# Stick-breaking attention with scanned products turned directly, steps of V, and scores in two row tiles

## The chip, the cores and the metric

One core of a Trainium2 chip runs one launch of the kernel. The metric is the device time in microseconds (us), lower is better. TensorE is called PE here, VectorE DVE, ScalarE ACT, GpSimd POOL, and SyncE SP. PSUM is the memory that PE writes to. It has eight banks of 512 float32 columns in 128 partitions.

## What is computed

One layer of a decoder for 2048 tokens of width 1024, float32: RMSNorm, a projection, two groups of attention heads, an output projection, a SwiGLU and a last RMSNorm. The change is in the second group, stick-breaking attention: 8 heads of 64, strictly causal.

```python
z = jnp.einsum('bqhd,bkhd->bhqk', qb, k) * scale
strict = key_idx[None, :] < q_idx[:, None]
log_beta = jax.nn.log_sigmoid(z)
log_1mb = jnp.where(strict, jax.nn.log_sigmoid(-z), 0.0)
later = lax.cumsum(log_1mb, axis=3, reverse=True) - log_1mb
a = jnp.where(strict, jnp.exp(log_beta + later), 0.0)
return jnp.einsum('bhqk,bkhd->bqhd', a, v)
```

With g = sigmoid(-z) and C[s] the product of g over all keys from s up to the query, the weight of key s is C[s+1] - C[s].

## The kernel before

Heads are worked in eight pairs p. Pairs 0 to 3 are the differential attention ("diff"), pairs 4 to 7 the stick-breaking one; m is 0 or 1, the head within a pair. A stick pair has 17 **pieces**. A piece is 128 queries by 1024 keys (or two query tiles that share 1024 columns), once for each m. A step e = 2i + m is one head of piece i, and the 68 pieces make 136 steps. For a step:

- `stick_scores` (L714, L716, L717) writes z into PSUM `h_z` m, in two banks of 512 columns. q and k are split in a high and a low part. k holds its high part in rows 0 to 63 and its low part in rows 64 to 127, and q holds one part in both halves of the rows, so a product over 128 rows by q high and one by q low give all four products. Where the diagonal lies in a run of columns, a 128-column product adds the mask.
- `gate` (ACT, L1096) turns z into sigmoid(-z) in place. `scan` (DVE, L1264) multiplies it up from the last key to the first, from PSUM into `h_more`. `difference` (POOL, L1364) writes C[s+1] - C[s] to `h_work`.
- `stick_turn` (L981) transposes the eight 128x128 tiles of `h_work` into `h_t`. `stick_evacuate` (ACT, L1105) copies them to `h_attn_t`. `stick_apply` (L1003) multiplies them with V into `h_o`, 64 output rows for each m.

After every fourth or fifth piece an output bank closes: `lift` (ACT), `lay` (PE, L1017), `settle` (ACT), `sum_squares` (DVE), `normalize_bank` (POOL).

Each engine runs a program of its own in a fixed order, and semaphores order them among each other. Around piece i PE does: scores of (i, m), turn of (i-2, m), half of the products with V of piece i-3, first for m = 0, then for m = 1. The scores of (i, m) wait until the scan of (i-1, m) has read `h_z` m.

In 11 of a pair's 17 pieces each bank holds one run of 512 columns. In the other six one bank holds two runs (384 and 128, or 256 and 256), as they belong to two query tiles: in three of them this is the upper bank, in three the lower. Ten of the eleven and all six hold a diagonal.

The diff part (units j) is another pipeline: PE scores, DVE `maximum` (L1178), ACT `exponential`, POOL `totals` (L1317), DVE `invert` (L1199), POOL `scale`, DVE `combine`, PE turn, ACT, PE apply. SP's queue loads the operands of pair p + 2 when pair p has been applied. `after(now)` runs side work of each engine at a given unit.

## Time and profile before

| what | value |
|---|---|
| median of 3 runs | 2861.14 us (2859.22 to 2863.82) |
| profiled execution: its own time, its span | 2860.66 us, 2858.8 us |
| PE busy | 2788.6 us, 98% of the span |
| DVE, ACT, POOL busy | 1894.1, 1471.7, 861.9 us |

The span is from the first to the last instruction of the profiled execution. Matmuls overlap in the array, so the busy time of PE includes overlap. A matmul takes weights that were loaded before it (PEld rows); the time that one costs is read from the start of one to the start of the next, not from its duration.

### The profile page before, as it was taken

What the parts mean: (1) busy time and instruction counts of PE and PEld (TensorE: products, weight loads), DVE (VectorE), ACT (ScalarE), POOL (GpSimd) and SP (SyncE); (2) the same over time, 40 slices, a digit from 0 to 9 for tenths busy, and PEclk for the clock granted to TensorE, in tenths of its full rate; (3) what the DMA queues carried; (4) which work ended last, traced back from release to release, by engine and by line L of the source; (5) the groups of instructions that cost most, each with busy time, mean ns of one, the idle gap of its engine ahead of it and who ended that gap; (6) DMA issues with size and microseconds to landing.
All of it is one profiled execution on the core that took longest, in us unless ns stands there. A gap on an engine that the chain in (4) does not pass through costs nothing.

```text
span 2858.8 us, 51825 instructions
## 1 busy us (share of the span) xinstructions
PE 2788.6 (98%) x19192; PEld 2449.8 (86%) x19192; DVE 1894.1 (66%) x2800; ACT 1471.7 (51%) x2572; POOL 861.9 (30%) x947
## 2 busy tenths in 40 slices
PE   7999999999999999999999999999999999999998
PEld 6888778878888877777899999998889998999886
DVE  6214430087777777777577877787478877878656
ACT  5112221177777666666455545554355555655444
POOL 1832222066776786776002221111100000011110
PEclk9999999999999999999999999999999999999999
DMA  5489897466554523520559999999757784899984
GB/s 195 137 191 225 211 231 170 119 156 148 113 133 107 119 60 75 119 82 16 199 164 331 323 284 289 283 285 290 197 165 235 241 252 157 256 328 300 253 230 158
DMA packets 303337, 559.42 MB, mean 196 GB/s; under 512 B 32272, under 2 KB 70160, under 8 KB 301968
## 3 DMA queue, kind: packets, MB, share of 16 engines
q1 hardware_dynamic: 262768, 463.06, 51.0%
q0 software_dynamic: 39072, 92.30, 17.4%
q8 instruction: 111, 1.82, 0.3%
q10 hardware_dynamic: 1312, 1.64, 0.2%
q14 instruction: 74, 0.61, 0.1%
HBM read 449.91 MB, written 197.13 MB: 226 GB/s over the span
## 4 chain that ended last, share of the span: by engine, by line
PE 70%; DVE 4%; DMA 2%; ACT 2%; issue 1%; POOL 1%; SPq 0%; DVEq 0%; ACTq 0%; POOLq 0%
PE f_ps L2507 26%; PE f_ps L2391 19%; PE h_z L714 5%; PE h_o L1003 5%; PE h_z L717 5%; PE h_t L981 4%; PE h_o L939 3%; PE h_t L924 2%; DVE f_wlo L1880 1%; DMA f_wraw<-sums_scratch 1%; PE h_z L716 1%; DVE h_negmax L1178 1%; PE f_ps L2431 0%; PE f_ps L2417 0%; DVE f_xsum L2093 0%
## 5 line engine op out<-in xcount | busy, mean ns | idle before, releaser
L1880 DVE TENSOR_TENSOR f_wlo<-f_wraw,f_whi 128x512 fp32r<-128x512 f32 x834 | 574.7, 690 | 234.1 <-ACT f_whi L1873 232.3
L1873 ACT ACTIVATE f_whi<-f_wraw 128x512 fp32r<-128x512 f32 x834 | 520.8, 627 | 393.8 <-PE f_ps L2507 254.3
L2507 PE MATMUL f_ps<-f_hi_s,f_whi 128*128 128x256 f32 x1408 | 391.2, 278 | 7.1 <-DVE f_up L2232 7.1
L2507 PE MATMUL f_ps<-f_lo_s,f_whi 128*128 128x256 f32 x1408 | 391.7, 278 | 0.0
L2507 PE MATMUL f_ps<-f_hi_s,f_wlo 128*128 128x256 f32 x1408 | 389.8, 277 | 0.0
L1364 POOL TENSOR_TENSOR h_work<-h_more 128x1024 f32<-128x1024 f32 (+7 forms) x192 | 264.7, 1395 | 115.6 <-DVE h_more L1264 115.6
L2507 PE MATMUL f_ps<-f_hi_a,f_whi 128*128 128x256 f32 x1056 | 292.0, 276 | 1.0 <-DVE f_second L2232 1.0
L2507 PE MATMUL f_ps<-f_hi_a,f_wlo 128*128 128x256 f32 x1056 | 291.6, 276 | 0.0
L2507 PE MATMUL f_ps<-f_lo_a,f_whi 128*128 128x256 f32 x1056 | 291.6, 276 | 0.0
L2507 PEld LDWEIGHTS f_ps<-f_hi_s,f_whi 128*128 128x128 f32 x1408 | 264.4, 188 | 8.8 <-DVE f_wlo L1880 4.4
L1264 DVE TENSOR_TENSOR_SCAN h_more<-h_z,h_zero 128x1024 f32<-128x1024 f32 (+7 forms) x128 | 231.7, 1812 | 59.4 <-ACT h_z L1096 56.9
L2507 PEld LDWEIGHTS f_ps<-f_hi_s,f_wlo 128*128 128x128 f32 x1408 | 264.8, 188 | 0.0
L2507 PEld LDWEIGHTS f_ps<-f_lo_s,f_whi 128*128 128x128 f32 x1408 | 264.4, 188 | 0.0
L1178 DVE TENSOR_REDUCE h_negmax<-h_z 128x1 f32<-128x1024 f32 (+7 forms) x192 | 169.5, 908 | 132.5 <-PE h_z L717 129.7
L2391 PE MATMUL f_ps<-f_whi,f_shi 128*128 128x512 f32 x608 | 237.3, 390 | 2.6 <-DVE f_slo L2209 2.6
L2391 PE MATMUL f_ps<-f_whi,f_slo 128*128 128x512 f32 x608 | 236.6, 389 | 0.0
L2391 PE MATMUL f_ps<-f_wlo,f_shi 128*128 128x512 f32 x608 | 236.6, 389 | 0.0
L714 PE MATMUL h_z<-h_k,h_qmain 128*128 128x512 f32 (+3 forms) x576 | 225.4, 399 | 6.9 <-ACT h_more L1050 3.9
L717 PE MATMUL h_z<-h_k,h_qmain 128*128 128x512 f32 (+3 forms) x576 | 222.0, 395 | 0.0
L1942 ACT ACTIVATE f_shi<-f_piece 128x512 fp32r<-128x512 f32 x154 | 97.4, 632 | 218.6 <-PE f_ps L2391 205.7
L1096 ACT ACTIVATE h_z<-h_z 128x1024 f32<-128x1024 f32 x136 | 137.0, 1008 | 135.1 <-PE h_z L717 135.0
L578 PE MATMUL p_ps<-p_hhi,p_whi 128*128 128x512 f32 x512 | 200.5, 392 | 1.8 <-DVE p_olo L502 1.8
(203 smaller groups left out, 6448.2 us busy)
## 6 DMA issues: line engine op xcount, KB each, us to landing
f_wraw<-in_w_stream SPq DMA_DIRECT2D x394, 256.0 KB, 4.3
f_wraw<-sums_scratch SPq DMA_DIRECT2D x352, 256.0 KB, 4.8
sums_scratch<-in_w_stream POOLq DMA_DIRECT2D x132, 256.0 KB, 5.4
act_scratch<-f_act SPq DMA_DIRECT2D x88, 256.0 KB, 4.0
combined_acts<-f_act SPq DMA_DIRECT2D x88, 256.0 KB, 5.2
f_wraw<-down_sums SPq DMA_DIRECT2D x88, 256.0 KB, 3.5
f_piece<-combined_acts SPq DMA_DIRECT2D x88, 256.0 KB, 3.1
down_sums<-in_w_stream POOLq DMA_DIRECT2D x66, 256.0 KB, 6.3
```

The lines of the kernel that those rows point to most:

```text
L578: mm = pe.matmul(bank[o % BLOCKS][:], w[s][:, c, :], h[:, c, :], start=(c == 0 and m == 0), stop=(c == KC - 1 and m == 2))
L714: pe.matmul(out, query(m, 0, seg["tile"]), keys, start=True, stop=False)
L717: mm = pe.matmul(out, query(m, 1, seg["tile"]), keys, start=False, stop=True)
L1003: mm = pe.matmul(o_bank[use % 2][own, at * P:(at + 1) * P], v_sb[s][:, seg["key_tile"] + j, own], attn_t[sticks[t["steps"][m]]["buf"]][:, ...
L1096: act.activation(z[e % 2][:], z[e % 2][:], ACT.Sigmoid, scale=-1.0).then_inc(S["gated"], 1)
L1178: done = dve.tensor_reduce(neg_max[R["set"]][:, col:col + 1], z[t["z"]][:, cols_of(seg)], AX.X, ALU.max, negate=True)
L1264: done = dve.tensor_tensor_scan(buffer[:, a:b][:, ::-1], z[m][:, cols_of(seg)][:, ::-1], zero[:].to_broadcast([P, seg["tiles"] * P]), begi ...
L1364: done = pool.tensor_tensor(work[sticks[e]["slot"]][:, cols_of(seg)], buffer[:, a + 1:b + 1], buffer[:, a:b], ALU.subtract)
L1873: act.activation(w_hi[ring][:], w_raw[ring][:], ACT.Copy).then_inc(S["hi_split"], 1)
L1880: dve.tensor_tensor(w_lo[ring][:], w_raw[ring][:], w_hi[ring][:].bitcast(F32), ALU.subtract).then_inc(S["lo_split"], 1)
L2391: mm = pe.matmul(bank[outs + t][:], a[:, tok], w[u % RING][:], start=(start and n == 0), stop=(stop and n == 2))
L2507: mm = pe.matmul(outs[i], w[ring][:, col], a[name][:, c, :], start=(c == 0 and m == 0), stop=(c == 3 and m == 2))
```

## The change

The weights are no longer formed. With V' [s] = V[s-1] - V[s] (V[-1] = 0) the sum over s of (C[s+1] - C[s]) V[s] is the sum over s of (C[s] - 1) V'[s]. So the scanned values are transposed as they are, the copy out of PSUM adds -1, POOL's `difference` is gone, and POOL makes V' once for each pair (`step_values`) from V and a copy of V that is loaded one row lower (`load_shifted`).

The gate writes to memory (`gated`), and the scan reads there. `h_z` has three slots of two banks instead of two and a separate `h_t`; scores and transposes take the slots in turn (`scores_in`, `turned_in`).

The scores of both heads of a piece are made together by products over 64 rows: head 0 in one half of the rows, head 1 in the other half (`load_crossed_keys` puts head 1's keys the other way round). Of the four partial products that of both low parts is left out, and three stay. For the third, each head changes to the other half of the rows, after a wait on the semaphore `crossed`.

PE's order around piece i is now: scores of piece i for both heads, turns of piece i-1 for both heads, `lay`, products with V of piece i-2 in one block.

```diff
+def load_crossed_keys(sp, k, qk_scratch, p, a, b, done):
+    row = rows_of(p)[1]
+    for m in range(2):
+        for part in range(2):
+            half = (part + m) % 2
+            sp.dma_start(k[half * HEAD_DIM:(half + 1) * HEAD_DIM, m, a:b].bitcast(F32),
+                         qk_scratch[part, row + m * HEAD_DIM:row + (m + 1) * HEAD_DIM, a:b]).then_inc(done, 16)
...
+def load_shifted(sp, v, v_scratch, p, done):
+    first = rows_of(p)[2]
+    rows = v_scratch[p // DIFF_PAIRS, :, first:first + COLS].rearrange("(k p) n -> p k n", p=P)
+    sp.dma_start(v[1:P], rows[0:P - 1]).then_inc(done, 16)
+    sp.dma_start(v[0:1, 1:TOK_TILES, :], rows[P - 1:P, 0:TOK_TILES - 1, :]).then_inc(done, 16)
...
+def groups_of(segs):
+    found = [[], []]
+    for bank in range(2):
+        runs = []
+        for seg in segs:
+            a, b = max(seg["at"], 4 * bank), min(seg["at"] + seg["tiles"], 4 * bank + 4)
+            if a < b:
+                first = seg["key_tile"] + a - seg["at"]
+                runs.append((seg["tile"], slice(a * P, b * P), slice(first * P, (first + b - a) * P), first + b - a == seg["tile"] + 1))
+        for n, run in enumerate(runs):
+            found[n].append((bank, run))
+    return found
...
+        scores_in, turned_in, held_by, place = {}, {}, [None, None, None], 0
+        for i in range(len(pieces) + 1):
+            for m in range(2):
+                if i < len(pieces):
+                    slot = m if i < 3 else place % 3
+                    scores_in[2 * i + m], held_by[slot] = (slot, held_by[slot]), ("gated", 2 * i + m + 1)
+                    place += 1
+            for m in range(2):
+                if i:
+                    slot = m if i < 3 else place % 3 if i < len(pieces) else 2
+                    turned_in[2 * (i - 1) + m], held_by[slot] = (slot, held_by[slot]), ("evacuated", 2 * (i - 1) + m + 1)
+                    place += 1
...
+        def stepped_at(p):
+            return diff_units + 1 + pieces_through(p - 2) + 6 if p > DIFF_PAIRS else units_through(p - 2) + 11
...
-                load_keys(sp, k_st[s], qk_scratch, p, HALF_SEQ, SEQ, late_keys[s])
-                load_keys(sp, k_st[s], qk_scratch, p, 0, HALF_SEQ, early_keys[s])
+                keys = load_keys if p < DIFF_PAIRS else load_crossed_keys
+                keys(sp, k_st[s], qk_scratch, p, HALF_SEQ, SEQ, late_keys[s])
+                keys(sp, k_st[s], qk_scratch, p, 0, HALF_SEQ, early_keys[s])
                 load_queries(sp, q_main[s], qk_scratch, p, INNER[1], LAST_TILE, INNER[1], outer[s])
                 load_queries(sp, q_main[s], qk_scratch, p, 0, INNER[0], 0, outer[s])
                 load_values(sp, v_sb[s], v_scratch, p, values[s])
+                if p >= DIFF_PAIRS:
+                    load_shifted(sp, v_step[s], v_scratch, p, values[s])
...
+                for e in t["steps"]:
+                    holder = scores_in[e][1]
+                    if holder is not None:
+                        pe.wait_ge(S[holder[0]], holder[1])
+                outs, keys, ends, rows = [ring[scores_in[e][0]] for e in t["steps"]], k_st[s], [None, None],                     (slice(0, HEAD_DIM), slice(HEAD_DIM, P))
+                def products(low, part, run):
+                    tile, cols, found, _ = run
+                    for m in range(2):
+                        own = rows[(m + low) % 2]
+                        ends[m] = pe.matmul(outs[m][:, cols], query_of(s)(m, part, tile)[own], keys[own, m, found],
+                                            start=not low and part == 0, stop=bool(low))
+                def masks(low, run):
+                    _, cols, _, diagonal = run
+                    for m in range(2 if diagonal else 0):
+                        own = rows[(m + low) % 2]
+                        pe.matmul(outs[m][:, cols.stop - P:cols.stop], ident_bf[own], strict[own], start=False, stop=False)
+                begun, (first, second) = t["crossed"], groups_of(t["segs"])
+                for _, run in first:
+                    products(0, 0, run)
+                    masks(0, run)
+                    products(0, 1, run)
+                    ends[1].then_inc(S["crossed"], 1)
+                for bank, run in first:
+                    pe.wait_ge(S["crossed"], begun + bank + 1)
+                    masks(1, run)
+                    products(1, 0, run)
+                    if second and second[0][0] == bank:
+                        ends[1].then_inc(S["crossed"], 1)
+                for _, run in second:
+                    pe.wait_ge(S["crossed"], begun + 3)
+                    products(0, 0, run)
+                    masks(0, run)
+                    products(0, 1, run)
+                    ends[1].then_inc(S["crossed"], 1)
+                    pe.wait_ge(S["crossed"], begun + 4)
+                    masks(1, run)
+                    products(1, 0, run)
+                for m in range(2):
+                    ends[m].then_inc(S["scored"], 1)
...
-                pe.wait_ge(S["multiplied"], e + 1)
-                if e:
-                    pe.wait_ge(S["evacuated"], e)
+                slot, holder = turned_in[e]
+                pe.wait_ge(S["scanned"], e + 1)
+                if holder is None:
+                    pe.wait_ge(D["evacuated"], diff_units)
                 else:
-                    pe.wait_ge(D["evacuated"], diff_units)
+                    pe.wait_ge(S[holder[0]], holder[1])
                 for j in range(CHUNK_TILES):
-                    mm = pe.transpose(t_bank[:, j * P:(j + 1) * P], work[step["slot"]][:, j * P:(j + 1) * P], ident[:])
+                    mm = pe.transpose(ring[slot][:, j * P:(j + 1) * P], work[step["slot"]][:, j * P:(j + 1) * P], ident[:])
...
-                cur, turning, applying, closing = piece_at(i), piece_at(i - 2), piece_at(i - 3), closing_at(i - 4)
-                if cur is None and turning is None:
-                    pe.wait_ge(S["scanned"], len(sticks))
-                    ahead()
+                cur, turning, applying, closing = piece_at(i), piece_at(i - 1), piece_at(i - 2), closing_at(i - 3)
+                if cur is not None:
+                    stick_scores(cur)
                 for m in range(2):
-                    if cur is not None:
-                        stick_scores(cur, m)
                     if turning is not None:
                         stick_turn(sticks[turning["steps"][m]])
-                    if applying is not None:
-                        stick_apply(applying, m)
-                    if m == 0 and closing is not None:
-                        lay(closing)
+                    if turning is pieces[-1] and m == 0:
+                        pe.wait_ge(S["evacuated"], len(sticks) - 2)
+                        ahead()
+                if closing is not None:
+                    lay(closing)
+                if applying is not None:
+                    stick_apply(applying)
...
-                act.activation(z[e % 2][:], z[e % 2][:], ACT.Sigmoid, scale=-1.0).then_inc(S["gated"], 1)
+                if e >= 2:
+                    act.wait_ge(S["scanned"], e - 1)
+                act.activation(gated[e % 2][:], ring[scores_in[e][0]][:], ACT.Sigmoid, scale=-1.0).then_inc(S["gated"], 1)
...
-                act.activation(attn_t[step["buf"]][:], t_bank[:], ACT.Copy).then_inc(S["evacuated"], 1)
+                act.activation(attn_t[step["buf"]][:], ring[turned_in[e][0]][:], ACT.Identity, bias=minus_one[:]).then_inc(S["evacuated"], 1)
...
-                m = e % 2
+                m, held = e % 2, work[sticks[e]["slot"]]
                 dve.wait_ge(S["gated"], e + 1)
-                if e >= 2:
-                    dve.wait_ge(S["multiplied"], e - 1)
+                if e >= 4:
+                    dve.wait_ge(S["transposed"], e - 3)
                 for seg in t["segs"]:
-                    buffer, a, b = shadow(seg, m)
                     begin = 1.0
                     if not seg["opens"]:
-                        begin = buffer[:, b:b + 1]
+                        begin = work[sticks[e - 2]["slot"]][:, 0:1]
                         dve.wait_ge(S["scanned"], e - 1)
-                    done = dve.tensor_tensor_scan(buffer[:, a:b][:, ::-1], z[m][:, cols_of(seg)][:, ::-1],
+                    done = dve.tensor_tensor_scan(held[:, cols_of(seg)][:, ::-1], gated[m][:, cols_of(seg)][:, ::-1],
                                                   zero[:].to_broadcast([P, seg["tiles"] * P]), begin, ALU.mult, ALU.add)
...
-            def difference(e, t):
-                if e >= 4:
-                    pool.wait_ge(S["transposed"], e - 3)
-                elif e == 0:
-                    pool.wait_ge(D["combined"], diff_units)
-                pool.wait_ge(S["scanned"], e + 1)
-                for seg in t["segs"]:
-                    buffer, a, b = shadow(seg, e % 2)
-                    done = pool.tensor_tensor(work[sticks[e]["slot"]][:, cols_of(seg)], buffer[:, a + 1:b + 1], buffer[:, a:b], ALU.subtract)
-                done.then_inc(S["multiplied"], 1)
+            def step_values(p):
+                s = p % 2
+                pool.wait_ge(values[s], 16 * DIFF_PAIRS // 2 + 48 * (p // 2 - DIFF_PAIRS // 2 + 1))
+                chain(pool.memset(v_step[s][0:1, 0, :], 0.0))
+                pool.tensor_tensor(v_step[s][:], v_step[s][:], v_sb[s][:], ALU.subtract).then_inc(S["stepped"], 1)
...
+                for p in range(DIFF_PAIRS, PAIRS_OF_MAPS):
+                    if stepped_at(p) == now:
+                        step_values(p)
```

PE's program, one half of a piece with its diagonal in a 128-column run, before (`h_t` is the transposes' PSUM, `h_o` the output bank):

```order
L714 MATMUL h_z<-h_k,h_qmain 128x512 [waits h_s_scanned]
L717 MATMUL h_z<-h_k,h_qmain 128x512
L714 MATMUL h_z<-h_k,h_qmain 128x384
L717 MATMUL h_z<-h_k,h_qmain 128x384
L714 MATMUL h_z<-h_k,h_qmain 128x128
L716 MATMUL h_z<-strict,ident_bf 128x128
L717 MATMUL h_z<-h_k,h_qmain 128x128
L981 MATMUL h_t<-ident_sb,h_work 128x128 [waits h_s_evacuated,h_s_multiplied]
L981 MATMUL h_t<-ident_sb,h_work 128x128 x7
L1003 MATMUL h_o<-h_attn_t,h_v 64x128 [waits h_o_copied,h_s_evacuated,h_values1]
L1003 MATMUL h_o<-h_attn_t,h_v 64x128 x7
```

In the changed kernel a whole piece of this kind stands like this; the rows end ahead of its last mask and product:

```order
L1033 MATMUL h_z<-h_k_49,h_qmain_52 128x512 [waits h_s_evacuated,h_s_gated]
L1033 MATMUL h_z<-h_k_49,h_qmain_52 128x512 x3
L1033 MATMUL h_z<-h_k_49,h_qmain_52 128x384 x4
L1033 MATMUL h_z<-h_k_49,h_qmain_52 128x512 [waits h_s_crossed]
L1033 MATMUL h_z<-h_k_49,h_qmain_52 128x512
L1033 MATMUL h_z<-h_k_49,h_qmain_52 128x384 [waits h_s_crossed]
L1033 MATMUL h_z<-h_k_49,h_qmain_52 128x384
L1033 MATMUL h_z<-h_k_49,h_qmain_52 128x128 [waits h_s_crossed]
L1033 MATMUL h_z<-h_k_49,h_qmain_52 128x128
L1040 MATMUL h_z<-strict,ident_bf 128x128 x2
L1033 MATMUL h_z<-h_k_49,h_qmain_52 128x128 x2
L1040 MATMUL h_z<-strict,ident_bf 128x128 [waits h_s_crossed]
```

Seven products and masks for each head have become 22 of half the rows for both heads, with four waits on `crossed` among them, of which the last two stand directly behind the product that they wait for. Behind the scores PE's rows are now these (turn, turn, apply):

```order
L1075 MATMUL h_z<-ident_sb,h_work 128x128 [waits h_s_evacuated,h_s_scanned]
L1075 MATMUL h_z<-ident_sb,h_work 128x128 x7
L1075 MATMUL h_z<-ident_sb,h_work 128x128 [waits h_s_gated,h_s_scanned]
L1075 MATMUL h_z<-ident_sb,h_work 128x128 x7
L1094 MATMUL h_o<-h_attn_t,h_vstep 64x128 [waits h_s_evacuated]
L1094 MATMUL h_o<-h_attn_t,h_vstep 64x128 x15
```

The second turn waits for `gated`, which before stood on no row of PE; each head's turn had its own apply behind it.

POOL's program in the last diff pair (p = 3), before:

```order
L1332 TENSOR_SCALAR h_more<-h_more,h_factor,h_neglam 128x1024
L1332 TENSOR_SCALAR h_more<-h_more,h_factor,h_neglam 128x512
L1332 TENSOR_SCALAR h_more<-h_more,h_inverse,h_neglam 128x512
L1311 TENSOR_TENSOR h_shift<-h_negall,h_negmax 128x4
L1317 TENSOR_TENSOR h_total<-h_sum,h_weight 128x4
L1318 TENSOR_TENSOR h_both<-h_total 128x2
L1324 TENSOR_TENSOR h_factor<-h_weight,h_inverse 128x4
```

and in the changed kernel:

```order
L1413 TENSOR_SCALAR h_more<-h_more,h_factor,h_neglam 128x1024
L1413 TENSOR_SCALAR h_more<-h_more,h_factor,h_neglam 128x512
L1413 TENSOR_SCALAR h_more<-h_more,h_inverse,h_neglam 128x512
L1392 TENSOR_TENSOR h_shift<-h_negall,h_negmax 128x4
L1442 MEMSET h_vstep 1x128
L1443 TENSOR_TENSOR h_vstep<-h_vstep,h_v_50 128x2048
L1398 TENSOR_TENSOR h_total<-h_sum,h_weight 128x4
L1399 TENSOR_TENSOR h_both<-h_total 128x2
L1405 TENSOR_TENSOR h_factor<-h_weight,h_inverse 128x4
```

Between the shift and the totals of one round now stand the clearing and the subtraction that make V' for pair 4.

## Rows read from the trace of the kernel before

**Rows 1.** The page: busy us (share of the span) and instructions of each engine.
```profile
PE 2788.6 (98%) x19192; PEld 2449.8 (86%) x19192; DVE 1894.1 (66%) x2800; ACT 1471.7 (51%) x2572; POOL 861.9 (30%) x947
```

**Rows 2.** Windows: stretch, its us, busy us (instructions) by engine, PE clock, DMA.
```profile
1100.00:1200.00 100.00, 100.00 (x941) 79.42 (x940) 74.13 (x47) 67.11 (x79) 70.24 (x57) 1.00 0.37 85
1200.00:1300.00 100.00, 100.00 (x949) 79.88 (x945) 75.32 (x48) 66.24 (x75) 72.61 (x59) 1.00 0.21 70
```

**Rows 3.** Timeline, half a piece without mask: start, us, engine, line, operation.
```profile
1136.89 0.50 PE L714 MATMUL h_z<-h_k,h_qlast 128*128 128x512 f32 x1
...
1137.23 0.40 PE L717 MATMUL h_z<-h_k,h_qlast 128*128 128x512 f32 x1
...
1137.69 0.39 PE L717 MATMUL h_z<-h_k,h_qlast 128*128 128x512 f32 x1
...
1137.92 1.04 PE L981 MATMUL h_t<-ident_sb,h_work 128*128 128x128 f32 x8
1138.12 1.01 ACT L1096 ACTIVATE h_z<-h_z 128x1024 f32<-128x1024 f32 x1 [1.07 <-PE h_z L717]
...
1138.89 0.85 PEld L1003 LDWEIGHTS h_o<-h_attn_t,h_v 128*64 128x64 f32 x16 [0.17 <-issue]
1138.89 1.09 PE L1003 MATMUL h_o<-h_attn_t,h_v 128*64 128x128 f32 x16
...
1139.17 2.35 DVE L1264 TENSOR_TENSOR_SCAN h_more<-h_z,h_more,h_zero 128x1024 f32<-128x1024 f32 x1 [0.73 <-ACT h_z L1096]
...
1139.91 0.50 PE L714 MATMUL h_z<-h_k,h_qlast 128*128 128x512 f32 x1
```

**Rows 4.** Timeline: short runs and their weight loads, the next two half pieces.
```profile
1120.63 0.19 PEld L714 LDWEIGHTS h_z<-h_k,h_qmain 128*128 128x128 f32 x1 [0.17 <-issue]
...
1120.74 0.19 PEld L717 LDWEIGHTS h_z<-h_k,h_qmain 128*128 128x128 f32 x1
...
1120.85 0.19 PEld L714 LDWEIGHTS h_z<-h_k,h_qmain 128*128 128x128 f32 x1
...
1123.89 0.50 PE L714 MATMUL h_z<-h_k,h_qmain 128*128 128x512 f32 x1
...
1127.05 0.50 PE L714 MATMUL h_z<-h_k,h_qmain 128*128 128x512 f32 x1
```

**Rows 5.** Timeline: from the last stick scores to the output projection.
```profile
1346.65 1.03 PE L981 MATMUL h_t<-ident_sb,h_work 128*128 128x128 f32 x8
...
1353.89 1.02 ACT L1105 ACTIVATE h_attn_t<-h_t 128x1024 f32<-128x1024 f32 x1 [0.21 <-PE h_t L981]
...
1355.06 1.06 PE L981 MATMUL h_t<-ident_sb,h_work 128*128 128x128 f32 x8 [0.18 <-ACT h_attn_t L1105]
...
1361.25 1.97 PE L1003 MATMUL h_o<-h_attn_t,h_v 128*64 128x128 f32 x32
...
1363.15 1.53 PE L2417 MATMUL f_ps<-ident_sb,f_natural 128*128 128x128 f32 x12
...
1364.87 0.49 PE L2391 MATMUL f_ps<-f_whi,f_thi 128*128 128x512 f32 x1
```

**Rows 6.** Timeline of POOL, then of DVE, in the last diff pair.
```profile
882.14 0.64 POOL L1311 TENSOR_TENSOR h_shift<-h_negall,h_negmax 128x4 f32<-128x4 f32 x1 [1.61 <-DVE h_negall L1185]
884.45 0.20 POOL L1317 TENSOR_TENSOR h_total<-h_sum,h_weight 128x4 f32<-128x4 f32 x1 [1.67 <-ACT h_weight L1074]
...
885.02 0.18 DVE L1199 RECIPROCAL h_inverse<-h_both 128x4 f32<-128x4 f32 x1 [0.39 <-POOL h_both L1318]
```

**Rows 7.** The load of V for pair 4, and a window behind its issue.
```profile
L700 SPq DMA_DIRECT2D h_v<-v_scratch x1: 597/597/597, 866.8 to 866.8; - x1
...
DMA to landing us min/median/max: 17.6/17.6/17.6
...
885.00:890.00 5.00, 5.00 (x39) 4.38 (x38) 3.98 (x5) 3.98 (x10) 3.95 (x4) 1.00 0.96 211
```

**Rows 8.** Groups by shape: POOL's `difference` at its largest size.
```profile
L1364 POOL TENSOR_TENSOR h_work<-h_more 128x1024 f32<-128x1024 f32 x80 | 151.2, 1893 | 74.4 <-DVE h_more L1264 74.4
```

114 lines of the change are left out of this document (47 added, 67 removed).

## The prediction

> **What bounds the kernel now.** I read the page first: PE is busy for 98% of the span [rows 1], so what PE does, or waits for, is the time. The windows say the same of the stretch that the change touches: from 1100 to 1300 us, in the middle of the stick phase, PE is busy without a gap and DVE for three quarters [rows 2]. POOL's `difference` is large there, but nobody on PE's path waits for it, so taking it away gives nothing by itself. The timeline then shows what PE's time consists of. In a half piece without a mask [rows 3] the first product begins at 1136.89, the second 0.34 later, the next two each 0.23 after that (1137.23 to 1137.69), the transposes at 1137.92, the sixteen products with V at 1138.89 and the next scores at 1139.91: 0.34 + 3 x 0.23 = 1.03 for scores, 0.97 to turn, 1.02 to apply, 3.02 in all. So a product of 512 columns costs 0.23, and the first one 0.11 more, which I call a switch. With a mask a half piece takes 3.16, one with a short run 3.26 [rows 4]; the mask is worth 0.13. In the same rows the weight loads of short runs start 0.11 apart: a run of 128 columns costs its load. PE is full, but a product's price is the larger of its columns and its load.
>
> **The change part by part.**
>
> *Scores, eleven full pieces of each pair.* Before, a piece makes 8 products of 512 columns, now 12 of half the rows. Nothing in the trace has two row tiles side by side, so a pair of them (one for each head) costs between 0.23, if they run together, and 0.46, if they don't. Two loads at 0.11 fill 0.22, so they fit under 0.23. I take 0.23, because the two use different rows and different PSUM. That is six pairs, 1.38. Add one switch 0.11 and two pairs of masks at 0.13 each, 0.26. The wait on `crossed` behind the second bank has one pair under it (0.23, from 0.11 on), while a product's duration is 0.39 and a handoff between engines 0.04 to 0.15 (below): 0.43 to 0.54 against 0.33, so it costs 0.1 to 0.2, say 0.15. Scores are 1.90 against 2 x (3.16 - 1.99) = 2.34 before.
>
> *Scores, six pieces with a short run.* Here each pair on a short run costs two loads, 0.22, whatever its columns. Three pairs of 512 are 0.69, six short pairs 1.32, masks 0.26, a switch 0.11. Where the short second run is in the upper bank, two waits on `crossed` come directly behind the product that they wait for, in the lower bank one. Such a wait empties the array: at least the 0.17 by which a product's duration exceeds its slot (0.40 - 0.23), at most that, the 0.15 of a handoff and a load of 0.11 twice, some 0.5. I take 0.35, as the handoff will count but not all loads. Upper: 2.38 + 0.10 + 0.70 = 3.18. Lower: 2.38 + 0.15 + 0.35 = 2.88. Before they took 6.32 to 6.52 for the whole piece, mean 6.42.
>
> *Turns.* The transposes and copies are as many as before, but the second turn gets the PSUM slot that head 0's scores have just been written to, so it waits for that gate. Nothing covers this but the first turn. From the start of head 0's last product: 0.39 until it has ended, 0.04 until the gate starts (1138.08 to 1138.12), 1.01 of gate [rows 3], 0.15 until PE starts (1354.91 to 1355.06 at the end of the phase [rows 5]), in sum 1.59. The first turn is through after 0.34 + 0.97 = 1.31, so PE idles 0.28. From the end of the scores to the end of the second turn it is 1.59 + 0.97 - 0.34 = 2.22 against 1.94.
>
> *Products with V.* 32 in one block take 1.90 (1361.25 to 1363.15 [rows 5]), against 2 x 1.02.
>
> *The sum of a piece.* Full with mask: 1.90 + 2.22 + 1.90 = 6.02 against 6.32, without mask 5.76 against 6.04, so -0.3 for each of eleven. Upper short run: 3.18 + 4.12 = 7.30 against 6.42, +0.88 for each of three. Lower: 7.00, +0.58 for each of three. For a pair -3.3 + 2.64 + 1.74 = +1.1, and **+4** for the four pairs.
>
> *What hides DVE and ACT.* Two scans at 2.35 are 4.7 [rows 3] beneath 5.76, so DVE is no bound; reading from memory where it read PSUM could even cost 20% (5.6). ACT's four passes of 1.02 are 4.1. The copy that adds -1 is the same pass. If PE fell to 4.7 per piece, DVE would be next.
>
> *V' for pair 4.* This stands on POOL in the diff phase, where it is not idle work. POOL has its shift done at 882.8 and begins the next totals at 884.45, and DVE's reciprocal waits for them 0.39 [rows 6]; DVE's maxima of the next round, and by them the exponentials and PE's scores, are queued behind it. In the changed program POOL must first have V and the shifted V. V is issued at 866.8 and lands 17.6 later, at 884.4; the shifted copy is 1.05 MB more at the 211 GB/s of that window [rows 7], 5.0 us, so 889.4. The subtraction of 2048 columns costs twice the 1.89 of 1024 [rows 8], 3.8. The totals then start at 893.2, 8.7 late, of which DVE has 0.4 to spare: **+8.4**. From below, if both land together, 3.3. From above, if the shifted V lands last (the window from 885 to 890 is still full, and 5 us come on top, 895), 14. For pairs 5 to 7 POOL waits likewise, but there only the normalizing of a bank stands behind it, which has some four pieces of time. The smaller, doubled key loads keep their bytes.
>
> *The end of the phase.* From the last scores' end, where the transposes start at 1346.65, to the first product of the output projection at 1364.87 it is 18.2 [rows 5]. With one piece less in flight what remains is: two turns 2.2, apply 1.9, a turn 1.0, the 16 transposes of the projection's input 1.9, a turn 1.0, two applies 3.8, 12 transposes 1.5, `lay` 0.5, in sum 13.8. **-4** (none to -6). The start of the phase is filled by the same units; I take nothing there.
>
> Together +4.3 + 8.4 - 4.4 = +8.3. The profiled execution took 2860.66, 0.5 below the median of the runs; I set 2869 for the median.
>
> **The rivals.** *Row tiles are cheaper than their bounds (faster).* If the loads of the two tiles overlap, a short pair costs 0.11 to 0.17, mean 0.14: 6 x 0.08 x 24 pieces = -12. If a wait on `crossed` costs only the 0.17, 36 of them give -6, and if the one in full pieces costs nothing, 68 x 0.15 = -10. All of it gives 2841, half of it 2855; I call this case 2850. It decides from about -14 on. Against it speaks that the sixteen loads of 64 columns in the column tiles of apply take 0.85 [rows 3], 0.05 each, one behind the other; for it, that those two use the same rows. The Trainium skill (TensorEngine Tiling (Array Packing), Key Properties) says that different tiles can execute loads and products in parallel. By that rule the short pairs alone would bring the sum to 2857; the apply rows disagree with it or are too short to show it. The same section says that a change of tiling mode drains the array, and the 0.11 of the first product [rows 3] agrees in kind.
>
> *Row tiles run one after the other (much slower).* A pair of 512 then costs 0.46. A pair of heads has 66 + 18 of them, +19.3, and the runs of 384 add 1.4: +83 for the phase, 2952. No row excludes it, since the column tiles' 0.06 per product fit both ways.
>
> *POOL's wait is not felt (no change).* If loads land earlier and DVE and PE have more slack than the row shows, only 0 to 3 of the 8.4 remain: 2861 to 2864.
>
> **How the numbers follow.** Forecast (2867 to 2890) 0.40, cheap tiles 0.32, serial tiles 0.10, hidden POOL wait 0.18. A measurement tells some 0.2% from no change, 5.7 us. Faster is the second case, 0.32. Same is the last one and the lower edge of the first, 0.20. Slower is the rest of the first and the third, 0.48. The range goes from the second case's all-in end, 2842, to the forecast with its upper costs (waits at 0.5: +5, POOL +6, switch and masks of row tiles dearer: +17), 2898. What it leaves out is the serial case and a little at both ends, 0.15 to 0.2. The forecast's own range is 2860 to 2885.
>
> **What the profile after would show.** Product pairs on L1033 start every 0.23 (0.46 would prove the serial case), short ones every 0.22. PE is idle some 0.3 before every second turn, released by the gate, and ACT's gate begins right behind the scores. Some 36 gaps of 0.2 to 0.5 stand before L1033 or L1040, released by PE itself. POOL's subtraction in pair 3 ends near 893, with a hole on DVE and PE of about 8 us there. The stick phase from the first gate to the last is some 4 us longer than before, and POOL is almost empty in it. I would be wrong if pairs cost clearly more or less than 0.23, if the second turn doesn't wait, or if the diff phase ends when it did.

## The result, and the profile after

The changed kernel takes 2973.52 us (median of 4 runs, 2970.29 to 2974.02) against 2862.48 (4 runs, 2859.22 to 2871.84): 1.038 times the time, interval 1.0354 to 1.0406. The profiled execution took 2973.34, with a span of 2971.5. Two anchors in the traces divide the 112.7 us between the spans. The first masked product of the stick phase (`strict`) starts at 912.50 before and at 973.21 after; the first product of the output projection starts at 1364.87 and at 1476.80. So the part ahead of the stick phase is 61 us longer, the stick phase 51 us (503.6 against 452.4), and the rest is equal within 1 us.

The page, first line of its busy times (share of the span, instructions):

```profile
PE 2779.8 (94%) x19640; PEld 2436.7 (82%) x19640; DVE 1896.9 (64%) x2797; ACT 1477.4 (50%) x2572; POOL 649.0 (22%) x763
```

PE is as busy as before within 9 us [rows 1], so what is new is idle time of PE. The windows (stretch, its us, busy us of each engine, PE clock, share of the DMA engines, GB/s) show the largest piece:

```profile
890.00:900.00 10.00, 0.53 (x5) 0.29 (x3) 0.00 (x0) 0.00 (x0) 0.00 (x0) 0.74 0.07 19
900.00:910.00 10.00, 0.00 (x0) 0.00 (x0) 0.00 (x0) 0.00 (x0) 0.00 (x0) 0.50 0.07 19
...
930.00:940.00 10.00, 0.00 (x0) 0.00 (x0) 0.00 (x0) 0.00 (x0) 1.53 (x2) 0.50 0.52 115
940.00:950.00 10.00, 3.43 (x14) 3.02 (x15) 4.84 (x7) 3.81 (x9) 7.45 (x7) 0.50 0.38 84
```

For some 40 us nothing runs but a transfer at 19 GB/s, with a DMA share of 0.07: one sixteenth is 0.0625, so one of the 16 engines is moving and fifteen are not. Before, the window behind the issue of V moved 211 [rows 7]. The timeline of the same place, first SP's queue, then POOL, then PE (start, us, engine, line, operation; the bracket is the idle time ahead and its releaser):

```profile
870.44 8.76 SPq L712 DMA_DIRECT2D h_vstep<-v_scratch  x1
879.25 54.35 SPq L713 DMA_DIRECT2D h_vstep<-v_scratch  x1
933.64 2.58 SPq L683 DMA_DIRECT2D h_qmain<-qk_scratch  x4
...
883.65 0.65 POOL L1392 TENSOR_TENSOR h_shift<-h_negall,h_negmax 128x4 f32<-128x4 f32 x1 [1.60 <-DVE h_negall L1274]
938.39 0.19 POOL L1442 MEMSET h_vstep<- 1x128 f32 x1 [54.09 <-DMA h_vstep<-v_scratch]
938.66 4.49 POOL L1443 TENSOR_TENSOR h_vstep<-h_vstep,h_v 128x2048 f32<-128x2048 f32 x1
943.11 0.20 POOL L1398 TENSOR_TENSOR h_total<-h_sum,h_weight 128x4 f32<-128x4 f32 x1
...
946.57 0.58 PE L733 MATMUL h_z<-h_k,h_qmain 128*128 128x256 f32 x1 [56.04 <-ACT h_more L1140]
```

L712 is the transfer of the shifted V over 127 partitions, L713 the small one over a single partition behind it. The second issue is held for 54.35 us. POOL, at L1442, waits in order for both; the totals of the last diff pair (L1398) stand behind it and start at 943.11 where they started at 884.45 [rows 6]. They release DVE's reciprocal, which releases the maxima, these the exponentials, and these at last PE's scores: PE is idle for 56.04 us. Four us into this idle time PE's granted clock falls from 2.4 to 1.2 GHz (0.50 in the windows), and it is back 6 us behind its end. The whole diff phase is 62 us longer than before.

The waits view from 920 to 1450 (who waits for whom: us in total, times, longest):

```profile
POOL h_vstep L1442 <- DMA h_vstep<-v_scratch: 137.5, 2, 83.4
...
POOL h_more L1442 <- DMA h_more<-v_scratch: 130.8, 2, 76.1
...
DVE h_ssumsq L1360 <- POOL h_out L1457: 55.5, 3, 37.0
PE h_z L1075 <- DVE h_work L1352: 49.2, 5, 33.1
...
PE h_z L1075 <- ACT h_more L1188: 13.6, 61, 1.2
```

The same happens to pairs 5, 6 and 7: POOL waits 76.1, 83.4 and 54.7 us for the shifted V. There it carries the normalizing of closed banks. The timeline before pair 6, on POOL, DVE and PE, shows who needed that:

```profile
1222.74 0.20 POOL L1442 MEMSET h_vstep<- 1x128 f32 x1 [83.37 <-DMA h_vstep<-v_scratch]
...
1230.88 0.69 DVE L1360 TENSOR_REDUCE h_ssumsq<-h_squares 128x8 f32<-128x512 f32 x1 [36.99 <-POOL h_out L1457]
1231.48 4.46 DVE L1352 TENSOR_TENSOR_SCAN h_work<-h_more,h_zero 128x1024 f32<-128x1024 f32 x2
...
1233.82 1.97 PE L1075 MATMUL h_z<-ident_sb,h_work 128*128 128x128 f32 x8 [33.09 <-DVE h_work L1352]
```

DVE's sum of squares of the next bank (L1360) must wait until the bank before is normalized, and the scans are queued behind it in order: PE stands still for 33.09 us. The periods from one piece's apply to the next are 6.0 to 6.8 us elsewhere; at these three places they are 21.1, 41.6 and 9.3 + 7.9, together 54 us too much.

Between these stalls the steady state can be read. A full piece with mask, then one with a short run in the upper bank, on PE:

```profile
1141.56 0.96 PE L1033 MATMUL h_z<-h_k,h_qmain 64*128 64x512 f32 x6
1142.37 0.23 PE L1040 MATMUL h_z<-strict,ident_bf 64*128 64x128 bf16 x2
...
1143.41 1.09 PE L1075 MATMUL h_z<-ident_sb,h_work 128*128 128x128 f32 x8
1144.69 1.06 PE L1075 MATMUL h_z<-ident_sb,h_work 128*128 128x128 f32 x8 [0.18 <-ACT h_more L1188]
1145.68 1.97 PE L1094 MATMUL h_o<-h_attn_t,h_more 128*64 128x128 f32 x32
1147.58 1.86 PE L1033 MATMUL h_z<-h_k,h_qmain 64*128 64x512 f32 x14
...
1149.80 0.23 PE L1040 MATMUL h_z<-strict,ident_bf 64*128 64x128 bf16 x2
...
1150.19 1.09 PE L1075 MATMUL h_z<-ident_sb,h_work 128*128 128x128 f32 x8
```

It answers to [rows 3, 4]. Scores 1.85, from their end to the end of the second turn 2.27, apply 1.90: 6.02. The short piece has 2.61 of scores. A whole pair, from the transposes of a closing to those of the same closing in the next pair, takes 107.4 us where no stall is in it; before it took 109.2.

### The profile page after: what moved, and what is told of

Read it like the earlier page. It is cut to its first block, busy times and chain, and to the rows that moved or that the text cites. A ratio compares the mean times of both kernels' runs of the same rounds, so it can differ in the third digit from the quotient of the medians.

```text
span 2971.5 us, 52610 instructions
## 1 busy us (share of the span) xinstructions
PE 2779.8 (94%) x19640; PEld 2436.7 (82%) x19640; DVE 1896.9 (64%) x2797; ACT 1477.4 (50%) x2572; POOL 649.0 (22%) x763
## 4 chain that ended last, share of the span: by engine, by line
PE 61%; another core or an unknown queue 7%; DVE 4%; ACT 3%; POOL 2%; issue 2%; DMA 1%; DVEq 0%; SPq 0%; ACTq 0%; POOLq 0%
PE f_ps L2585 26%; PE f_ps L2469 18%; PE h_o L990 3%; PE h_o L1094 3%; PE h_z L1033 3%; PE h_z L736 2%; PE h_z L733 2%; PE h_z L1075 2%; PE h_z L975 2%; ACT h_more L1188 1%; DVE h_work L1352 1%; DVE f_wlo L1958 1%; DMA f_wraw<-in_w_stream 1%; DVE h_negmax L1267 1%
## 5 line engine op out<-in xcount | busy, mean ns | idle before, releaser
L1352 DVE TENSOR_TENSOR_SCAN h_work<-h_more,h_zero 128x1024 f32<-128x1024 f32 (+7 forms) x128 | 233.0, 1844 | 46.4 <-ACT h_more L1188 46.4
L1188 ACT ACTIVATE h_more<-h_z 128x1024 f32<-128x1024 f32 x136 | 132.3, 1022 | 181.0 <-PE h_z L1033 124.1
L1075 PE MATMUL h_z<-ident_sb,h_work 128*128 128x128 f32 x1088 | 151.4, 284 | 64.6 <-DVE h_work L1352 49.2
L2585 PEld LDWEIGHTS f_ps<-f_hi_a,f_whi 128*128 128x128 f32 x1056 | 198.3, 188 | 3.3 <-DVE f_wlo L1958 1.1
L578 PE MATMUL p_ps<-p_hlo,p_whi 128*128 128x512 f32 x512 | 199.3, 389 | 0.0
```

Of the source, the lines that this page charges most:

```text
L578: mm = pe.matmul(bank[o % BLOCKS][:], w[s][:, c, :], h[:, c, :], start=(c == 0 and m == 0), stop=(c == KC - 1 and m == 2))
L1075: mm = pe.transpose(ring[slot][:, j * P:(j + 1) * P], work[step["slot"]][:, j * P:(j + 1) * P], ident[:])
L1188: act.activation(gated[e % 2][:], ring[scores_in[e][0]][:], ACT.Sigmoid, scale=-1.0).then_inc(S["gated"], 1)
L1352: done = dve.tensor_tensor_scan(held[:, cols_of(seg)][:, ::-1], gated[m][:, cols_of(seg)][:, ::-1], zero[:].to_broadcast([P, seg["tiles"] ...
L2585: mm = pe.matmul(outs[i], w[ring][:, col], a[name][:, c, :], start=(c == 0 and m == 0), stop=(c == 3 and m == 2))
```

## The experiments

Times of single executions of one kernel differ by more than 20 us: the ten of e4_shift_128_later go from 2860.39, with a mean granted clock of 0.996, to 2883.71 with 0.990. Where PE runs at a lower clock differs between the traces, also where the programs are still alike: from 560 to 600 us the mean granted clock is 1.00 before and in e5, 0.91 in the changed kernel and in e4, and 0.87 in e1. So below each median stands with its ratio to before, measured at the same time, and edits in the stick phase are compared by the trace as well: by the time of a pair (as above, 17 pieces without a stall), and by the whole stick phase between the two anchors.

| kernel | median us (runs) | ratio to before, 95% | stick phase | a pair |
|---|---|---|---|---|
| before | 2862.48 (4) | 1 | 452.4 | 109.2 |
| after | 2973.52 (4) | 1.038 (1.0354 to 1.0406) | 503.6 | 107.4 |
| e1_shift_by_128 | 2876.24 (6) | 1.0044 (1.0017 to 1.0071) | 456.6 | 107.4 |
| e2_shift_112_15 | 2877.06 (1) | | 457.6 | |
| e3_127_from_0 | 2979.80 (1) | | | |
| e4_shift_128_later | 2869.71 (10) | 1.0031 (1.0014 to 1.0049) | 461.9 | 107.4 |
| e5_full_rows | 2854.08 (10) | 0.9973 (0.995 to 0.9995) | 442.8 | 103.5 |
| e6_apply_between | 2855.88 (10) | 0.9991 (0.9972 to 1.0009) | 442.6 | 103.6 |
| e8_step_late | 2925.76 (1) | | 455.1 | |
| e9_high_first | 2853.75 (10) | 0.9963 (0.9948 to 0.9979) | 452.7 | 104.5 |
| e7_in_parts | 2837.93 (5) | 0.9916 (0.9887 to 0.9944) | 432.2 | 103.5 |
| e10_slot_sooner | 2853.89 (10) | 0.9973 (0.9959 to 0.9988) | 443.8 | |
| e11_row_tiles_mended | 2833.21 (6) | 0.9903 (0.9879 to 0.9927) | 423.7 | 100.7 |
| e12_full_rows_mended | 2837.36 (6) | 0.9907 (0.9892 to 0.9923) | 433.9 | 102.7 |

**Why is the transfer slow?** My theory was the number of partitions; the rivals were the small transfer, the source's offset by a row, and the start at partition 1. e1_shift_by_128 takes tiles 1 to 15 over all 128 partitions:

```
-    sp.dma_start(v[1:P], rows[0:P - 1])
-    sp.dma_start(v[0:1, 1:TOK_TILES, :], rows[P - 1:P, 0:TOK_TILES - 1, :])
+    low = v_scratch[p // DIFF_PAIRS, P - 1:SEQ - 1, first:first + COLS].rearrange("(k p) n -> p k n", p=P)
+    sp.dma_start(v[:, 1:TOK_TILES, :], low)
+    sp.dma_start(v[1:P, 0:1, :], rows[0:P - 1, 0:1, :])
```

> The changed kernel, with only the shifted load of V in another cut: tiles 1 to 15 as one transfer over all 128 partitions, tile 0 as one over 127 partitions (65 KB). Theory A, from the trace after: the transfer over 127 partitions (1.04 MB) runs on one of the 16 DMA engines, because 127 rows aren't shared out; it moves 19 GB/s at a DMA share of 0.07, which is 1/16, and takes some 60 us. Then here the large one runs at over 200 GB/s (5 us), the small one takes 3 to 4 us, POOL's wait for pair 4 shrinks from 54 to some 8 us, those for pairs 5 to 7 reach PE no longer, and the total falls by 95 to 110 us to 2862 to 2876. Rival B: the transfer into one partition (7.5 KB) is what is slow, SP is held 54 us at it; then this falls as well, so the next run must tell. Rival C: reading V a second time, at an address one row off, is slow in itself; then this stays near 2973.

e2_shift_112_15 leaves the small transfer alone and splits the large one into 112 and 15 partitions:

```
-    sp.dma_start(v[1:P], rows[0:P - 1])
+    sp.dma_start(v[1:P - 15], rows[0:P - 16])
+    sp.dma_start(v[P - 15:P], rows[P - 16:P - 1])
```

> The changed kernel, the transfer over partitions 1 to 127 cut in two: 112 partitions (7 x 16) and 15; the one into partition 0 stays as it is. Theory A: 112 partitions are shared by all engines (0.9 MB, 5 us), 15 are not (0.12 MB on one engine, 6 us), the total falls to 2865 to 2885. Rival B (the transfer into one partition is slow): it stays near 2973. Rival C (source one row off): near 2973. A rival D, that starting at partition 1 is slow: near 2973.

e3_127_from_0 keeps 127 partitions, but from partition 0 on and from an unshifted source:

```
-    sp.dma_start(v[1:P], rows[0:P - 1])
-    sp.dma_start(v[0:1, 1:TOK_TILES, :], rows[P - 1:P, 0:TOK_TILES - 1, :])
+    sp.dma_start(v[0:P - 1], rows[0:P - 1])
+    sp.dma_start(v[P - 1:P], rows[P - 1:P])
```

> The changed kernel with the shift left out of the copy of V: 127 partitions from partition 0 on, then partition 127 by itself, so V' is zero and the stick heads are wrong; all else is as before. Theory A (127 is not shared out): the large transfer again takes 50 to 60 us and the total stays at 2965 to 2980. Rival D (a start at partition 1 is slow) or C (an address one row off): the total falls to 2862 to 2885.

The first two are rid of the slow transfer (2876.24, a fall of 97 us that ends just at the upper edge of what I expected, and 2877.06), the third, which leaves out the shift, is not (2979.80). A window of e3, columns as above:

```profile
900.00:910.00 10.00, 0.00 (x0) 0.00 (x0) 0.00 (x0) 0.00 (x0) 0.00 (x0) 0.50 0.07 19
```

Still 19 GB/s. Neither the start, nor the source, nor the small transfer counts, only the 127. Both 128 and 112 + 15 partitions are fast: from 880 to 890 us, with V and the shifted V on their way, e2 moves 187 and 223 GB/s in its two windows of 5 us and e1 262 and 302. The Trainium skill states it (DMA: Bandwidth & Descriptors, section on why a DMA increments its semaphore by 16): the number of engines is the largest one up to 16 that divides the outermost sizes, and it names 127 partitions as a case of one engine. All three runs and the share of 0.07 agree. By the same rule 15 partitions are shared out too, over 15 engines, and not held on one, as I had expected for e2; no run here tells the two apart. I had not weighed the rule in the prediction.

In e1 POOL still waits, as the timeline at pair 4 shows:

```profile
887.77 0.65 POOL L1393 TENSOR_TENSOR h_shift<-h_negall,h_negmax 128x4 f32<-128x4 f32 x1 [1.59 <-DVE h_negall L1275]
895.92 0.20 POOL L1443 MEMSET h_vstep<- 1x128 f32 x1 [7.50 <-DMA h_vstep<-v_scratch]
896.20 4.50 POOL L1444 TENSOR_TENSOR h_vstep<-h_vstep,h_v 128x2048 f32<-128x2048 f32 x1
900.65 0.20 POOL L1399 TENSOR_TENSOR h_total<-h_sum,h_weight 128x4 f32<-128x4 f32 x1
```

The shift is done at 888.4, V' at 900.65, the totals follow. That is the case for which the prediction had its 8.4.

**Where should V' of pair 4 stand?** e4_shift_128_later is e1 with this subtraction moved behind the diff phase's last unit:

```
-            return ... if p > DIFF_PAIRS else units_through(p - 2) + 11
+            return ... if p > DIFF_PAIRS else diff_units
```

> The first of these runs, and V' for pair 4 is made on POOL in unit 68 (the end of the differential part) in place of unit 62. By my prediction the wait and the subtraction in unit 62 cost 8.4 us there, so this run is 6 to 10 us faster than the first one and ends at 2854 to 2866. Rival: with the load repaired the subtraction's place does not matter, POOL's lateness is taken up by slack, and the two agree within 3 us.

The median falls by 6.5, but it ends at 2869.71, above the 2854 to 2866 that I expected, and the intervals of the two ratios overlap, so the times alone don't decide between the theory and its rival. The traces do so for the diff phase: from its first masked product (`causal`) to the anchor it has 349.7 us against 360.3 in e1, PE's wait of 9.4 us is gone, and the longest that is left is 2.2. But the stick phase of e4 is 5.3 longer than that of e1: the subtraction now meets the first scan, which takes 5.70 us where it has 2.29 in e1 (more at e7). So part of the cost has moved there. The 349.7 are still 9.5 more than before (340.2). This isn't V' but the clock of this execution: from 560 to 850 us PE is at half clock for 20.4 us, which costs it half of them, against 3.4 before, and e5, with the same program in this phase but for the form of the key loads, has 341.1.

**Does the slow transfer hurt by itself for pairs 5 to 7, or only by POOL's order?** e8_step_late is the changed kernel with its slow transfer, where POOL is sent to the subtraction eight pieces later:

```
-            return diff_units + 1 + pieces_through(p - 2) + 6 if p > DIFF_PAIRS else ...
+            return diff_units + 1 + pieces_through(p - 2) + 14 if p > DIFF_PAIRS else ...
```

> The changed kernel as it was, with the slow transfer over 127 partitions left in, and one change: for pairs 5 to 7 GpSimd is sent to the subtraction at the 14th piece of the pair ahead instead of the 6th. Theory A, the transfer is harmful there only because GpSimd waits for it 76 and 83 us in order, with the normalizing of closed banks queued behind, which then holds VectorE's scans: the stalls of TensorE ahead of pairs 5, 6 and 7 (about 15, 35 and 4 us) all but go, the 56 us of pair 4 stay, and the time is 2915 to 2932. Theory B, the loss comes from the transfer itself (it fills one DMA queue, and loads behind it come late): the time stays within 10 us of 2973.

2925.76 in its one execution: theory A. The waits of PE for the diff exponentials (pair 4, as before) and for the scans:

```profile
PE h_z L733 <- ACT h_more L1140: 57.5, 1, 57.5
...
PE h_z L1075 <- DVE h_work L1352: 3.9, 4, 1.2
```

The 49.2 us that PE waited for scans are 3.9, the stick phase is 455.1, 48.5 shorter. The transfer takes as long as it did; nobody is queued behind it.

**What do the row tiles bring?** e5_full_rows is e4 with the old scores (all else of the change stays):

```
-                keys = load_keys if p < DIFF_PAIRS else load_crossed_keys
+                keys = load_keys
...
-                (products(), masks() and the waits on S["crossed"])
+                for m in range(2):
+                    score_matmuls(pe, ring[scores_in[t["steps"][m]][0]], query_of(s), k_st[s], m, t["segs"],
+                                  (ident_bf, strict)).then_inc(S["scored"], 1)
```

> The kernel of e4 (shifted copy over 128 partitions, V' of pair 4 later) with the scores of the stick-breaking pairs done as before the change: four products of 128 rows for each head and bank instead of six of 64 rows in two row tiles, keys loaded uncrossed, no waits on the crossing. Everything else of the change stays. Read from periods between the first apply products of neighbouring pieces: e4 has 6.02 us for a full piece, 6.67 for one with a short run in the upper bank, 6.45 to 6.47 with one in the lower bank, and 107.2 for a whole pair. Theory A, row tiles are where the steady gain comes from and the rest of the rebuilding gives nothing in steady state: full piece 6.22 (before 6.31, and the scores of two halves were 2.06 there against 1.86 now), lower short run 6.2 to 6.3, a pair 109 +-0.4, and the time 5 to 10 us above e4. Theory B, row tiles are eaten up by the waits at the crossings and the gain comes from blocks of 16 transposes and 32 applies: full piece 6.02 or less, short runs about 6.1, a pair under 107, the time below e4.

Theory A falls: the ratio drops by 0.6%, with intervals that do not overlap, and a pair from 107.4 to 103.5. The numbers are those of theory B. A full piece with mask on PE:

```profile
1167.65 0.50 PE L734 MATMUL h_z<-h_k,h_qmain 128*128 128x512 f32 x1
...
1169.55 0.48 PE L737 MATMUL h_z<-h_k,h_qmain 128*128 128x512 f32 x1
1169.86 1.91 PE L1040 MATMUL h_z<-ident_sb,h_work 128*128 128x128 f32 x16
1171.70 1.97 PE L1059 MATMUL h_o<-h_attn_t,h_vstep 128*64 128x128 f32 x32
1173.60 0.50 PE L734 MATMUL h_z<-h_k,h_qmain 128*128 128x512 f32 x1
```

Scores are 2.21, 0.36 more than with row tiles. But the turn is one row of 16 without a wait, 1.84, where it was 2.27: now head 0's scores are ready 1.1 us before head 1's, so its gate runs beneath head 1's products. With row tiles both heads are ready only at the end, and the second turn waits. The full piece is 5.95 against 6.02, and pieces with a short run are 5.97 to 6.18 against 6.44 to 6.78: six such pieces, times half a microsecond, are most of the 3.9 of a pair. So the waits at the crossings, to which theory B gave the whole loss, explain the short pieces (e9 tests it), and the wait for the gate explains the full ones (e6 tests it). In the changed kernel the row tiles lose, and the rest of the rebuilding (blocks of transposes and applies, one less piece in flight) gives 109.2 - 103.5 = 5.7 us a pair; no run divides it among these.

**The two kinds of waits of the row tiles.** e6_apply_between is e4 with apply between the two turns:

```
                 for m in range(2):
                     if turning is not None:
                         stick_turn(sticks[turning["steps"][m]])
...
-                if closing is not None:
-                    lay(closing)
-                if applying is not None:
-                    stick_apply(applying)
+                    if m == 0 and closing is not None:
+                        lay(closing)
+                    if m == 0 and applying is not None:
+                        stick_apply(applying)
```

> The kernel of e4 with one change in the order on the TensorE queue: transposes of head 0, then the apply of the piece before (and the closing transposes), then transposes of head 1. In e4 the transposes of head 1 wait 0.17 to 0.18 us of idle time for the gate in 60-odd pieces. Theory A, that wait is only a matter of order: with 1.9 us of apply ahead of the second transposes it goes, a full piece takes 5.8 instead of 6.02, and the kernel is 10 to 15 us faster than e4. Theory B, it only moves, since the scores of the next piece need the buffer that the second transposes free late and the ScalarE queue is in its old order: full piece 6.0 or more, time within 3 us of e4 or above.

Theory A: the ratio falls by 0.4% to 0.9991, some 11 us. The turn of head 1 has no bracket any more:

```profile
1170.26 1.97 PE L1095 MATMUL h_o<-h_attn_t,h_vstep 128*64 128x128 f32 x32
1172.16 1.09 PE L1076 MATMUL h_z<-ident_sb,h_work 128*128 128x128 f32 x8
1173.18 0.97 PE L1034 MATMUL h_z<-h_k,h_qmain 64*128 64x512 f32 x6
```

The second turn starts 1.90 behind the products with V, with no wait between. A full piece takes 5.80, a pair 103.6 instead of 107.4.

e9_high_first is e4 with the high products of all runs first, then the low ones:

```
                 for n, (bank, run) in enumerate(runs):
                     products(0, 0, run, banks.index(bank) == n)
                     masks(0, run)
                     products(0, 1, run)
                     ends[1].then_inc(S["crossed"], 1)
                 for n, (bank, run) in enumerate(runs):
                     pe.wait_ge(S["crossed"], begun + len(banks) - banks[::-1].index(bank))
                     masks(1, run)
                     products(1, 0, run, bank not in banks[n + 1:])
```

> The kernel of e4 with another order of the score products where a bank holds two runs: the high products of all runs first, then the low ones (the start flag is then set at the first run of a bank alone), so that two of the four waits on the crossing go. It touches 6 of 17 pieces of a pair; full pieces keep their order. Theory A, the excess of pieces with a short run over full ones (0.65 us in the upper bank, 0.43 in the lower, of which closing banks are no part) is mostly those two waits of 0.27 to 0.31: it falls by 0.4 to 0.6, a pair by 2.5 to 3.5 us, the kernel by 8 to 14 us against e4. Theory B, the excess is the narrow products themselves, which cost 0.2 for 128 columns about as for 512: it falls by less than 0.15 and the time stays within 3 us of e4.

Theory A again. From the start of a short piece's scores to its turn:

```profile
1174.96 1.08 PE L1034 MATMUL h_z<-h_k,h_qmain 64*128 64x512 f32 x10
...
1176.91 1.09 PE L1067 MATMUL h_z<-ident_sb,h_work 128*128 128x128 f32 x8
```

That is 1.95 for a piece with two runs of 256 columns in the upper bank, where the same piece has 2.51 in e4. Its period falls from 6.67 to 6.12, only 0.10 above a full one, so each of the two waits was worth 0.28. And the masks being as many as in a full piece, three pairs of 512 columns (0.69) and 0.10 pay for six pairs of 256: 0.13 for such a pair, below the 0.22 of two loads [rows 4]. The loads of the two row tiles overlap. The Trainium skill says so (TensorEngine Tiling (Array Packing), Key Properties), and with the waits out of the way the trace agrees. The medians fall by 16 us, more than the 11.6 that four pairs of 2.9 give and than the 8 to 14 that I expected; no run tells where the rest comes from.

**Why do pieces last 2 to 4 us longer while POOL subtracts?** In e5 three pieces take 7.20, 8.82 and 8.78 us, where their like in other pairs have 5.95, 6.39 and 6.40, so 6.1 us in all (the 6.7 in the expectation below compares two of them with pieces of another kind). POOL and DVE at the first of them:

```profile
975.43 0.19 POOL L1407 MEMSET h_more<- 1x128 f32 x1 [33.37 <-DMA h_more<-v_scratch]
975.71 4.71 POOL L1408 TENSOR_TENSOR h_more<-h_more,h_v 128x2048 f32<-128x2048 f32 x1
...
977.96 3.54 DVE L1317 TENSOR_TENSOR_SCAN h_work<-h_more,h_work,h_zero 128x512 f32<-128x512 f32 x1 [1.92 <-ACT h_more L1153]
...
982.54 1.25 DVE L1317 TENSOR_TENSOR_SCAN h_work<-h_more,h_work,h_zero 128x512 f32<-128x512 f32 x1
```

The scan of 512 columns, 1.25 us at 982.54, takes 3.54 and ends about when the subtraction does. Before, `difference` ran beside the scans, and of the 72 scans of 1024 columns with that form none took more than 2.29; but that scan read PSUM. e7_in_parts is e5 with the subtraction in eight parts:

```
-                pool.tensor_tensor(v_step[s][:], v_step[s][:], v_sb[s][:], ALU.subtract).then_inc(S["stepped"], 1)
+                for part in range(8):
+                    own = slice(2 * part, 2 * part + 2)
+                    done = pool.tensor_tensor(v_step[s][:, own, :], v_step[s][:, own, :], v_sb[s][:, own, :], ALU.subtract)
+                done.then_inc(S["stepped"], 1)
```

> The kernel of e5 with GpSimd's subtraction of a pair (128x2048) cut into eight of 128x256. In the profile of e5 the scans of VectorE that run while GpSimd subtracts take 4.3 to 4.4 us longer than their like (in e4: 5.80 for 128x640 against 1.46, 8.81 for two of 128x1024 against 4.47), and the pieces there last 7.20, 8.82 and 8.78 us where the others of their kind have 5.96, 5.97 and 6.17: 6.7 us in all. Theory A, one instruction with two inputs from memory on VectorE and one on GpSimd exclude each other for as long as an instruction lasts: in parts a scan waits for at most one part, about 0.6 us, the three long pieces shrink to within 0.7 of their like, and the time falls by 4 to 7 us. Theory B, both only share a rate, or the eight parts each take a turn with the scan held: the long pieces stay within 1 us of what they were. On before the scan had one input from memory and one from PSUM, so neither is seen there.

```profile
973.78 9.73 POOL L1410 TENSOR_TENSOR h_more<-h_more,h_v 128x256 f32<-128x256 f32 x8
...
976.38 1.78 DVE L1317 TENSOR_TENSOR_SCAN h_work<-h_more,h_work,h_zero 128x512 f32<-128x512 f32 x1 [1.91 <-ACT h_more L1153]
978.09 1.69 DVE L1317 TENSOR_TENSOR_SCAN h_work<-h_more,h_zero 128x512 f32<-128x512 f32 x1
```

Now each scan of 512 columns takes 1.7 to 1.8, half a microsecond for one part, and the eight parts take 9.73 where one instruction took 4.71: they take turns. The three long pieces are 6.05, 6.39 and 6.40, and the head of the phase, where the subtraction for pair 4 met the first scans (8.74 us for two), is 4.7 shorter. The stick phase falls by 10.6 us, more than I expected, since I had not counted the head. The ratio falls by 0.6%, some 16 us, of which the trace shows these 10.6. The Trainium skill has the rule (SBUF — State Buffer, section on the two separate sides): VectorE with two operands from SBUF and GpSimd hold one pair of ports in turn, each for a whole instruction. The traces agree in both directions: POOL's multiplications of 256 columns (`h_out` by `h_srstd`) all take 0.61 us before; in e4 their mean is 1.83 and the longest takes 2.59. This is what "scan from memory" cost, and the prediction had looked for it in the scan's own duration, where it isn't (2.29 us for 1024 columns where POOL is quiet, as before).

**The head of the phase.** e10_slot_sooner is e5 with the ring's third buffer used from piece 2 on:

```
-                    slot = m if i < 3 else place % 3
+                    slot = m if i < 2 else place % 3
```

> The kernel of e5 with the third PSUM buffer given to the transposes one piece sooner at the head of the stick-breaking phase (the turns of piece 1 go to it instead of waiting for the gates of piece 2). In e5 TensorE waits 4.70, 0.25, 0.15 and 2.27 us in the first four pieces, and then runs at half clock for some us. Theory A, the ring of only two buffers in these pieces makes the head long: the 2.27 goes and the head is 2 to 4 us shorter, the time as much. Theory B, the 2.27 is the wait of ScalarE's evacuation for the last apply of the difference attention (5.18 us there), which this does not touch, and the 4.70 is the scan of piece 0: within 1.5 us of e5 in the head.

In the head theory A holds in part: the wait of 2.27 is not gone but 1.4, and the second period 9.41 instead of 11.97, so from the anchor to the second apply 31.8 us instead of 35.0. The long wait at its start (4.70) does not change. ScalarE in e5 shows what it is:

```profile
917.83 1.02 ACT L1153 ACTIVATE h_more<-h_z 128x1024 f32<-128x1024 f32 x1 [4.08 <-DVE h_work L1317]
```

The gate of piece 1 waits 4.08 us for the scan of piece 0, whose buffer it needs. In the median nothing is seen (2853.89 against 2854.08), where 2 to 4 us less were expected: its profile has 4.1 us more in the pieces with a subtraction, so the times cannot tell 2 or 3 us here.

**All of it together.** e11_row_tiles_mended has the edits of e4, e6, e7, e9 and e10; e12_full_rows_mended has them with the old scores (so without e9).

> All of the change kept, row tiles too, with the mended edits together: shifted copy over 128 partitions, V' of pair 4 later, high products first, apply between the two transposes, the subtraction in eight parts, the third buffer a piece sooner. From the traces: e6 has 103.6 us for a pair and e9 took 0.55 us off each of six pieces of it, so 100.3 to 100.8 for a pair against 109.1 before and 105.9 for e5 with 128-row scores. Theory A, the savings add, since each goes at a wait of its own on TensorE: 2825 to 2842. Theory B, with these waits gone VectorE's scans (some 75 to 78 us busy of 100) or ScalarE's order set the pace: a pair of 102.5 or more and 2843 to 2856.

> The kernel of e11 with the scores as before the change (four products of 128 rows for each head and bank, no row tiles, no waits on the crossing), all else alike: what the row tiles are worth once the waits around them are gone. In e7, with 128-row scores and transposes of both heads in a row, a full piece takes 5.95 us and a pair 103.5; e11 has 5.80 and 100.7. Theory A, in the order with apply between the transposes 128-row scores change nothing, since there was no gate wait left to cover: a pair 103.2 to 103.7, and 6 to 12 us above e11, so the row tiles are worth 0.15 us for a full piece. Theory B, the gain of e11 over e7 is the order alone: a pair 101 or less, and the time within 3 us of e11.

e11 has theory A: 2833.21, 0.9903 of before. A piece whose closing follows:

```profile
1134.73 0.96 PE L1034 MATMUL h_z<-h_k,h_qmain 64*128 64x512 f32 x6
...
1136.57 1.09 PE L1067 MATMUL h_z<-ident_sb,h_work 128*128 128x128 f32 x8
...
1138.03 1.97 PE L1086 MATMUL h_o<-h_attn_t,h_vstep 128*64 128x128 f32 x32
1139.93 1.09 PE L1067 MATMUL h_z<-ident_sb,h_work 128*128 128x128 f32 x8
```

A full piece takes 5.80 and a pair 100.7: 107.4 - 3.8 (e6) - 2.9 (e9) = 100.7, so the savings add. In e12 a pair takes 102.7, between my two theories: the order gives 0.8 to the old scores too, and the row tiles are worth 2.0 us a pair, 8 for the four. The stick phases of the traces differ by 10.2 (433.9 and 423.7), the rest lying in the head and where scans meet subtractions. The medians differ by 4 and the intervals of the ratios overlap, so the whole times alone don't show it.

## Why the prediction was wrong, step by step

**The step that failed** is in "V' for pair 4": "the shifted copy is 1.05 MB more at the 211 GB/s of that window [rows 7], 5.0 us, so 889.4". I took the rate of a window full of other transfers for a transfer of another shape. It measured 54 to 59 us at 19 GB/s, and the wait on PE 56.0 in place of 8.4. From the same number follows the second half of the error: "for pairs 5 to 7 POOL waits likewise, but there only the normalizing of a bank stands behind it, which has some four pieces of time". With a fast transfer it held: in e1 POOL still waits there, up to 36 us, and PE stands for scans 5.5 us in all. With 83 us of wait it did not, and behind the normalizing stood DVE's next sum and behind that the scans: 54 us. That 56 and 54 make 110 of the 111 us between the medians is partly luck, as 8.4 of the 56 were forecast and the other terms below nearly cancel. What the transfer cost is read from e1, which differs from the changed kernel in it alone: 97 us. e1 has 2876.24, within 8 us of the forecast and within its range.

**V' for pair 4, with a transfer that all engines share**, was priced about right: PE waits 9.4 us in e1, against 8.4. Its subtraction takes 4.50 where I had 3.8.

**Scores in full pieces:** 1.85 against my 1.90. A pair of row tiles runs together, at 0.23; the serial case fell. **The turn:** 2.27 against 2.22, with the wait for the gate as told, a bracket of 0.18 beside later starts. **Apply:** 1.90 as told. The whole piece was 6.02, as computed; without mask 5.86 against 5.76.

**Short runs** were mis-sized: 2.50 to 2.61 of scores in the upper bank and 2.28 to 2.44 in the lower, against 3.18 and 2.88. A short pair of 256 columns costs 0.13 (e9), not 0.22; a wait on `crossed` 0.28, not 0.35. So the steady state was 1.8 us a pair faster, -7.3 for four in place of +4. This was the first rival's mechanism: some 11 of the 28 us that it had listed.

**The end of the phase:** from the last scores to the projection 15.1 us (1461.74 to 1476.80) against 18.2; I had 13.8. -3.1 in place of -4.4.

**The start of the phase**, where I took nothing, was mis-sized as well: the apply of the second piece starts 33.0 us behind the anchor in e1, 27.2 before. e1's stick phase is 4.2 longer than before; with -7.3 for the steady part, -3.1 for the end and +6.5 for the three collisions of subtraction and scan, some +8 are left for it. In the trace of e1 PE waits 6.0 us there against 2.3 before, and it is granted half clock for 10.3 us against 3.4, of which half is lost: 3.7 and 3.4 us, together 7 of the 8. The collisions themselves stand in no term.

So that e1 comes near the sum is luck: its steady state is 11 us better than told, and a head and collisions of 15 us were not told at all.

**What the profile after would show:** right for the 0.23 of pairs, PE's bracket ahead of each second turn and POOL nearly empty; wrong for the end of the subtraction (943, not 893), for the hole (56, not 8) and for the stick phase (51 us longer, not 4). The gaps at the crossings stand before weight loads of PEld, not before products: from 920 to 1450 us there are 60, 16 us in all, the longest 0.5.

## What to carry to other kernels

Read the shape of a new transfer before its bytes: a load over 127 partitions ran at 19 GB/s with the share of one engine in 16, and the same bytes over 128, or over 112 and 15, did not. Ask of every wait that is moved to an idle engine what stands behind it in order, and for how long it can stand: for pairs 5 to 7 the same slow transfers cost 49 us or nothing, by the place of one wait. And where a step makes two results ready at once instead of one after the other, count who worked on the first beneath the second: the row tiles saved 0.36 us of products and lost 0.43 in the turn behind them, until the order was turned.

## What the runs showed of the hardware

- A transfer over 127 partitions ran at 19 GB/s with a DMA share of 0.07, from partition 0 as well as from partition 1 (after, e3), and over 128 or 112 + 15 partitions at the rate of the rest, 187 to 302 GB/s in the windows from 880 to 890 (e1, e2).
- A scan with its inputs in memory and a POOL operation with two inputs in memory exclude each other for an instruction's length: 3.54 us for 1.25 (e5), 5.80 for 1.46 (e4); with the subtraction in eight parts each scan loses about 0.5 and POOL takes twice as long (9.73 for 4.71, e7). With the scan's input in PSUM neither was seen: 2.29 for 1024 columns and 0.61 for POOL's 256 (before).
- Two products of 64 rows in two row tiles cost as much as one (0.23 for 512 columns), and a pair of 256 columns 0.13, so their weight loads overlap (e9). A wait that orders two row tiles on one bank costs PE 0.28 where it stands directly behind the product that it waits for.
- Ten executions of one kernel (e4) spread over 23 us; the fastest has a mean granted clock of 0.996, the slowest of 0.990. In the idle time of 56 us PE's clock fell to 0.50 (after).
